# Row lists of 32 experts built in one scatter instead of one one-hot sum per expert

## The chip, the cores and the metric

One core of one Trainium2 chip runs the whole program in one launch. The metric is the device time of the program in microseconds; 1805.8 us is the median of three runs of the kernel before (1805.31 to 1807.24).

## The reference

`reference` is two blocks over 512 tokens of width 1024. The first is a mixer (mLSTM heads and pooling) with a mixture of experts behind it, the second an attention block with spatial gating. The change touches the mixture of experts alone:

```python
logits = (xt @ w_router + b_router).astype(jnp.float32)
top_vals, top_idx = lax.top_k(logits, TOP_K)          # 4 of 32 experts
top_gates = jax.nn.softmax(top_vals, axis=-1)
...
def expert_block(args):
    xb, e = args
    gate = xb @ w_gate[e] + b_gate[e]
    up = xb @ w_up[e] + b_up[e]
    gate = jnp.minimum(gate, SWIGLU_LIMIT)
    up = jnp.clip(up, -SWIGLU_LIMIT, SWIGLU_LIMIT)
    glu = gate * jax.nn.sigmoid(SWIGLU_ALPHA * gate)
    return (glu * (up + 1.0)) @ w_down[e] + b_down[e]
```

Each token's four results are weighted by `top_gates` and summed. Every expert has three 1024 x 1024 float32 matrices, 12 MB in all.

## The kernel before

**Turns.** The experts are sorted by their number of rows, and `vector_order` gives each a place, so that turns alternate between a larger expert (even turn, up to 128 rows) and a smaller one (odd turn, `small(e)`, up to 64 rows). What does not fit is left to `further_blocks`. Turn `e` has 12 pieces of weights of 1 MB: 8 for gate and up, and 4 for down of the expert before.

**A piece.** SyncE loads it into one of five ring slots (`load`, L447) once ScalarE and VectorE have read what was there. ScalarE writes its high part to `WH` (`high`, L1042), VectorE its low part to `WL` (`low`, L1386: ring minus WH, both in SBUF). There are five such pairs of buffers; a buffer is free when TensorE has used it. TensorE multiplies high by high, high by low and low by high; in smaller turns it packs high and low rows into one pass (`rows_by_columns`).

**Rows.** `h2d` in memory holds the 512 normed tokens. `gpsimd_gather(e)` fetches the rows of turn `e` by an indirect DMA into `xg[e % 2]`, with indices from `tok`. TensorE transposes them (`tensor_turn_rows(e)`, L755), ScalarE and VectorE keep them as `xh` and `xl`. `gpsimd_scatter(e)` writes the results by `dst` to `yd`, which has one row for every token and choice.

**Lists of rows.** `P1[token, e]` is the place of the token in the expert's list, plus one, or zero. For a turn `q`, `vector_one_hot(q)` compares `P1` with a row of numbers (four instructions for four blocks of 128 tokens), `tensor_index(q, bank)` multiplies the result with `DV16` (four matmuls of one column, which sum 4 x token + choice + 1), and `vector_index(q, bank)` makes `dst` and `tok` from the sum. Turns 0 to 2 (NI = 3) are done ahead of the loop or in turn 0; later ones, for turn `e + 3`, within turn `e`: the one-hot at piece 2, the matmuls at piece 4 (bank 7, behind a wait for the low part of the transposed hidden rows), the indices at piece 5.

**Order.** Every engine has its own order of instructions, written out by hand; semaphores tie them together. TensorE's is, from the start of the loop: gate and up of turn 0, rows of turn 1, gate and up of turn 1, rows of turn 2, down of turn 0, hidden rows of turn 1, and so on (`tensor_experts`, L875). GpSimd's is (`gpsimd_experts`, L2042): gather 0, biases 0, gather 1, zero and copy `selz`, biases 1 to 3, gather 2, gather 3, scatter 0, gather 4, scatter 1 and so on. VectorE's start is in `vector_experts` (L1716): two low parts with the positions and the one-hots between, the count of what does not fit, the weights `GK`, the fifth low part, then the turns.

Of the kernel before, what the change touches and what calls it, by code (L numbers as in the profile page):

```python
# [73 lines left out]
def program(nc, x, norm1_g, w_in, ig_b, fg_b, conv_w, head_norm_g, pool_w, pool_scale, w_out, norm2_g,  # L74
# [40 lines left out]
    dst = place("dst", [128, E], I32)  # L115
    tok = place("tok", [128, E], I32)
    wc = place("wc", [128, 16], F32)
    fl = place("fl", [128, 16], F32)
    ovm = place("ovm", [128, E, 3], F32)
# [16 lines left out]
    h2d = nc.dram_tensor("h2d", [T, D], F32).ap()  # L136
    b3d = nc.dram_tensor("b3d", [2, 3, E, D], BF16).ap()
    yd = nc.dram_tensor("yd", [T * K, D], F32).ap()
    xv = x[0].rearrange("(j p) d -> p j d", p=128)
    yv = yd.rearrange("(j p k) d -> j p k d", p=128, k=K)  # L140
    ov = out[0].rearrange("(j p) d -> j p d", p=128)
# [88 lines left out]
    bf = ordering("bf", [128, 4], F32)  # L230
    bidx = ordering("bidx", [128, 4], I32)
    foldw = ordering("foldw", [128, HALF], F32R)
    WH += [reg(f"WH{3 + i}", [128, 4, 512], F32R, 53.5 + 16 * i) for i in range(2)]
    WL += [reg(f"WL{3 + i}", [128, 4, 512], F32R, 61.5 + 16 * i) for i in range(2)]

# [185 lines left out]

    t_rows = {e: max(0, 2 * e - 1) for e in range(E)}
    t_mid = {e: 2 * e + 2 if e + 1 < E else 2 * e + 1 for e in range(E)}
    NI = 3
    small = lambda e: e % 2 == 1
    places = lambda e: HALF if small(e) else 128
    fold = {}
# [343 lines left out]

    def tensor_turn_rows(e):
        P.wait_ge(s_xg[e % 2], 16 * (e // 2 + 1))
        P.wait_ge(s_ix, min(e + NI, E) if e else 1)
        if e:
            P.wait_ge(s_tl, t_rows[e])
        else:
            P.wait_ge(s_tall, 16)
        if e == 2:
            P.wait_ge(s_spk, 1)  # L780
        tensor_turn8(xg[e % 2], places(e))
# [34 lines left out]
    def tensor_gate_up(e):  # L816
        P.wait_ge(s_th, t_rows[e] + 1)
        for p in range(8):
            which, kc = p // 4, p % 4
            if p == 0:  # L820
                if e == 0:
                    P.wait_ge(s_lg, 2)
                    P.wait_ge(s_x1, 8)
                else:
                    P.wait_ge(s_eg, e)
            last = rows_by_columns(n_g[e] + p, kc, 2 * which, xh, xl, 0 if p else t_rows[e] + 1, small(e))
            if p == 3:

                if e:
                    P.wait_ge(s_eu, e)  # L830
                else:
                    P.wait_ge(s_bh, 112)
                    P.wait_ge(s_cnt, 1)
                if e == 1:
                    P.wait_ge(s_selz, 2)
                if e == 8:
                    P.wait_ge(s_bh, 160)
                for n in range(4):
                    rows = slice(32 * n, 32 * n + 24)
                    cols = selz[rows, e % 8 // 2] if small(e) else sel8[rows, e % 8:e % 8 + 1].broadcast_to([24, 128])  # L840
                    last = mm(PS[:, n, :], cols, b3[rows, e // 8], n >= 2, n < 2)
            last.then_inc(s_mm, 1)
            if small(e) and p == 1 and e >= 3:
                P.wait_ge(s_low, fold["out", e - 2])
                tensor_fold(4, ysl).then_inc(s_fold, 1)
            if small(e) and p == 6:
                P.wait_ge(s_low, fold["gate", e])
                tensor_fold(0, egl).then_inc(s_fold, 1)
            if p == 1 and e == 1:
                tensor_turn_mid(0)  # L850
            if e == 0 and p + 1 < NI:
                tensor_index(p + 1, 4 + p)
            if p == 4:
                P.wait_ge(s_tl, t_mid[e - 1] + 1 if e else 1)
                if e + NI < E:
                    tensor_index(e + NI, 7)
                if e == 1:
                    P.wait_ge(s_sp, 1)
                    for j in range(4):
                        last = P.transpose(PS[0:32, 6, 128 * j:128 * j + 128], Gt[:, j], ident)  # L860
                    last.then_inc(s_spt, 1)

    def tensor_down(e):
        P.wait_ge(s_th, t_mid[e] + 1)
# [760 lines left out]
        vector_order()  # L1625

    def vector_order():
        V.wait_ge(s_small, 128)
        V.scalar_tensor_tensor(key, cnt, 32.0, late[:, KEYB:KEYB + E], MUL, ADD).then_inc(dv.sem, dv.one())
        for i in range(4):  # L1630
            V.wait_ge(dv.sem, dv.n)
# [26 lines left out]
    def vector_positions():  # L1658
# [3 lines left out]
        V.tensor_copy(cnt, PS[:, 4, 128:160]).then_inc(dv.sem, dv.one())  # L1662
        V.wait_ge(dv.sem, dv.n)

    def vector_further_count():
        V.tensor_tensor(key, cnt, late[:, ADJ:ADJ + E], ADD).then_inc(dv.sem, dv.one())
        V.wait_ge(dv.sem, dv.n)
# [6 lines left out]
        V.tensor_copy(novi, nov[:, 0:1]).then_inc(s_nov, 1)  # L1674

    def vector_one_hot(q):
        if q >= NI:
            V.wait_ge(s_im, q - NI + 1)
        n = places(q)
        for j in range(4):  # L1680
            last = V.tensor_scalar(oh[q % NI][:, j, 0:n], iot16[:, 0:n], P1[:, j, q:q + 1], None, ALU.is_equal)
        last.then_inc(s_oh, 1)

    def vector_index(q, bank):
# [4 lines left out]
        V.scalar_tensor_tensor(dst[0:n, q:q + 1], PS[0:n, bank, 0:1], -1.0, iv[0:n, 0:1], ADD, ADD).then_inc(dv.sem, dv.one())  # L1689
        V.wait_ge(dv.sem, dv.n)  # L1690
        V.tensor_scalar(tok[0:n, q:q + 1], dst[0:n, q:q + 1], 2, None, ALU.arith_shift_right).then_inc(s_ix, 1)  # L1691

    def vector_turn8(t, hi, lo, e):
        V.wait_ge(s_th, t + 1)
# [21 lines left out]
    def vector_experts():  # L1716
# [4 lines left out]
        for q in range(1, NI):  # L1721
            vector_one_hot(q)
        low(first + 3)
        vector_further_count()
        V.wait_ge(s_ek, 1)
        V.reciprocal(sm, sm).then_inc(dv.sem, dv.one())
# [5 lines left out]
        for e in range(E + 1):  # L1732
            if e < E:
                for p in range(8):
# [279 lines left out]
    def gpsimd_routing():  # L2014
        G.tensor_copy(tri16[:, 0], C[:, LTRI:LTRI + 128])
        G.tensor_copy(tri16[:, 1], C[:, ONES:ONES + 128]).then_inc(s_tri, 1)
        G.wait_ge(s_sc, 4)
        G.dma_start(late, cst[:, NC1:NCST]).then_inc(s_small, 16)
        G.tensor_copy(foldw, C[:, IDENT + HALF:IDENT + 128]).then_inc(s_selz, 1)

    def gpsimd_gather(e):
        i = e % 2
        G.wait_ge(s_ix, e + 1)
        if e >= 2:
            G.wait_ge(s_tt, t_rows[e - 2] + 1)
        n = places(e)
        G.indirect_dma_start(xg[i][0:n], None, h2d, bass.IndirectOffsetOnAxis(tok[0:n, e:e + 1], 0), bounds_check=T - 1,  # L2027
                             oob_is_err=False).then_inc(s_xg[i], 16)

    def gpsimd_biases(g):  # L2030
        G.wait_ge(s_sig, 2)
# [4 lines left out]
    def gpsimd_scatter(e):  # L2036
        G.wait_ge(s_ys, e + 1)
        n = places(e)
        G.indirect_dma_start(yd, bass.IndirectOffsetOnAxis(dst[0:n, e:e + 1], 0), ys[e % 2][0:n].rearrange("p h f -> p (h f)"), None,  # L2039
                             bounds_check=T * K - 1, oob_is_err=False).then_inc(s_y[e % 2], 16)  # L2040

    def gpsimd_experts():  # L2042
# [248 lines left out]
```

## Time and profile before

| | us |
|---|---|
| median of three runs | 1805.8 |
| the profiled execution, whole | 1807.08 |
| its span | 1805.7 |
| TensorE matmuls busy | 1684.4 (93%) |
| VectorE busy | 1380.5 (76%) |
| ScalarE busy | 1212.3 (67%) |
| GpSimd busy | 229.4 (13%) |
| VectorE low parts (L1386), 428 | 966.3 |
| ScalarE high parts (L1042), 428 | 814.2 |
| GpSimd gathers of rows (L2027), 32 | 75.3 |
| GpSimd scatters of results (L2039), 32 | 94.6 |

The profile is of one execution, times in microseconds from the start of the span. Its engines are PE (TensorE matmuls), PEld (TensorE weight loads), DVE (VectorE), ACT (ScalarE), POOL (GpSimd) and SP (SyncE, which issues the weight loads). `x32` is a count. `A <- B` behind a wait means that B released A. PEclk is the clock that TensorE was granted, as a share of its full speed. The chain is the work that ended last, followed back from the end of the program. The expert loop runs from about 235 to 1363 us; the mixer lies before it, the second block behind it.

### The profile page before, as it was taken

To read this page: it belongs to the slowest core of one execution; us is meant where nothing else is said; L and a number is where in the kernel's file an instruction comes from. 1 tells how busy PE (TensorE), PEld (TensorE's weight loads), DVE (VectorE), ACT (ScalarE), POOL (GpSimd) and SP (SyncE) were. 2 spreads that over 40 slices of the span, in tenths; PEclk is the share of its full clock that TensorE was granted. 3 is DMA by queue.
4 is the path that set the end of the run, shared out by engine and by line. 5 is a ranking of instruction groups with operands and counts; after the bars stand their busy time and mean duration, and the time that the engine had idled before them with its cause. 6 is when DMAs were issued, how large, how long until landed. Compare 5 with 4: busy or idle time off the path is not lost.

```text
span 1805.7 us, 20193 instructions
## 1 busy us (share of the span) xinstructions
PE 1684.4 (93%) x7609; PEld 1258.7 (70%) x7609; DVE 1380.5 (76%) x1226; ACT 1212.3 (67%) x931; POOL 229.4 (13%) x143
## 2 busy tenths in 40 slices
PE   7999879999999998998989998999988999999998
PEld 5777757676676676676766766766753777778887
DVE  4567689899899989988989998999875524775343
ACT  4354458888888878878888888888873346664232
POOL 1411031022021011210120130122001000000000
PEclk9999979999999999999999999999997999999999
DMA  7311369999999999999999999999985422122221
GB/s 273 126 47 72 134 245 369 393 378 381 388 385 368 376 364 368 386 373 377 355 379 390 367 373 380 364 371 389 378 326 214 140 70 71 47 76 94 94 82 47
DMA packets 94003, 487.99 MB, mean 270 GB/s; under 512 B 12056, under 2 KB 13776, under 8 KB 43984
## 3 DMA queue, kind: packets, MB, share of 16 engines
q1 hardware_dynamic: 81696, 462.64, 67.2%
q0 software_dynamic: 8000, 18.25, 2.8%
q10 hardware_dynamic: 4208, 5.77, 0.9%
q8 instruction: 62, 1.02, 0.2%
q14 instruction: 37, 0.30, 0.0%
HBM read 477.97 MB, written 17.17 MB: 274 GB/s over the span
## 4 chain that ended last, share of the span: by engine, by line
PE 58%; DVE 19%; DMA 8%; issue 8%; ACT 7%; SPq 0%; DVEq 0%; ACTq 0%; POOLq 0%
PE PS L516 52%; DVE WL L1386 12%; DMA ring<-in_w_down_dram 7%; ACT WH L1042 4%; DVE eu L1708 2%; DVE eu L1714 2%; PE PS L977 1%; PE PS L755 1%; DMA ring<-in_w_gate_dram 1%; PE PS L989 1%; ACT eg L1211 1%; ACT eul L1195 1%; DVE xl L1698 1%; DVE xh L1696 1%; PE PS L628 0%
## 5 line engine op out<-in xcount | busy, mean ns | idle before, releaser
L1386 DVE TENSOR_TENSOR WL<-ring,WH 128x2048 fp32r<-128x2048 f32 x428 | 966.3, 2284 | 242.7 <-ACT WH L1042 242.5
L1042 ACT ACTIVATE WH<-ring 128x2048 fp32r<-128x2048 f32 x428 | 814.2, 1913 | 294.1 <-PE PS L516 246.7
L516 PE MATMUL PS<-WH,xh 128*128 128x512 f32 x1024 | 309.1, 403 | 2.2 <-DVE xh L1696 1.5
L516 PE MATMUL PS<-WL,xh 128*64 128x512 f32 (+1 forms) x1024 | 300.9, 398 | 0.0
L516 PEld LDWEIGHTS PS<-WH,xh 128*128 128x128 f32 x1024 | 187.8, 190 | 52.7 <-issue 7.2
L516 PEld LDWEIGHTS PS<-WL,xh 128*64 128x64 f32 (+1 forms) x1024 | 164.0, 164 | 72.4 <-issue 9.0
L2039 POOL DMA_INDIRECT yd<-ys,dst x32 | 94.6, 2956 | 924.3 <-ACT ys L1223 924.3
L516 PE MATMUL PS<-WH,hh 128*128 128x512 f32 x512 | 156.9, 408 | 1.5 <-DVE hh L1696 1.5
L516 PE MATMUL PS<-WL,hh 128*64 128x512 f32 (+1 forms) x512 | 149.4, 399 | 0.0
L516 PE MATMUL PS<-WH,xl 128*128 128x512 f32 x512 | 140.4, 397 | 0.0
L516 PEld LDWEIGHTS PS<-WH,hh 128*128 128x128 f32 x512 | 94.7, 192 | 30.9 <-issue 7.4
L516 PEld LDWEIGHTS PS<-WH,xl 128*128 128x128 f32 x512 | 98.8, 193 | 21.5
L516 PE MATMUL PS<-h,WH 128*128 128x512 f32 x288 | 113.3, 394 | 0.0
L516 PE MATMUL PS<-l,WH 128*128 128x512 f32 x288 | 112.2, 389 | 0.0
L516 PE MATMUL PS<-h,WL 128*128 128x512 f32 x288 | 112.1, 389 | 0.0
L516 PEld LDWEIGHTS PS<-WL,hh 128*64 128x64 f32 (+1 forms) x512 | 84.5, 165 | 33.3
L2027 POOL DMA_INDIRECT xg<-h2d,tok x32 | 75.3, 2353 | 28.0 <-DVE tok L1691 16.2
L516 PE MATMUL PS<-WH,hl 128*128 128x512 f32 x256 | 71.1, 401 | 0.0
L516 PEld LDWEIGHTS PS<-h,WH 128*128 128x128 f32 x288 | 54.1, 188 | 11.7 <-issue 0.2
L516 PEld LDWEIGHTS PS<-h,WL 128*128 128x128 f32 x288 | 54.1, 188 | 11.4
L516 PEld LDWEIGHTS PS<-l,WH 128*128 128x128 f32 x288 | 54.1, 188 | 10.8
L755 PE MATMUL PS<-C,eu 128*128 128x128 f32 (+1 forms) x256 | 38.0, 290 | 22.2 <-DVE eu L1714 12.0
(385 smaller groups left out, 2158.0 us busy)
## 6 DMA issues: line engine op xcount, KB each, us to landing
ring<-in_w_gate_dram SPq DMA_DIRECT2D x128, 1024.0 KB, 8.5
ring<-in_w_up_dram SPq DMA_DIRECT2D x128, 1024.0 KB, 7.1
ring<-in_w_down_dram SPq DMA_DIRECT2D x128, 1024.0 KB, 8.0
ring<-in_w_in_dram SPq DMA_DIRECT2D x32, 1024.0 KB, 5.4
ring<-in_w_out_dram SPq DMA_DIRECT2D x8, 1024.0 KB, 5.0
yk<-yd SPq DMA_DIRECT2D x4, 1024.0 KB, 7.9
X<-in_x_dram SPq DMA_DIRECT2D x4, 512.0 KB, 9.7
h2d<-HV ACTq DMA_DIRECT2D x4, 512.0 KB, 2.8
```

Source lines behind the costliest of these rows:

```text
L516: return P.matmul(ps, a, b, start=start, stop=stop)
L755: last = P.transpose(PS[:, 6 + at_ // 512, at_ % 512:at_ % 512 + n], pairs_[0:n, k // 2, k % 2], ident[0:n, 0:n])
L977: last = P.matmul(flat[:, OFF[i] + 128 * (i2 - i):OFF[i] + 512 - 128 * i], tri[:, 0 if i2 == i else 1], part[:, OFF[i2]:OFF[i2] + 512 - 12 ...
L989: last = P.matmul(flat[:, OFF[i]:OFF[i] + 512 - 128 * i], kT[r0:r0 + 64, ch, 128 * i:128 * i + 128], nq[r0:r0 + 64, ch, 128 * i:512], star ...
L1042: A.activation(WH[buf[n]], ring[spot[n]], ACT.Copy).then_inc(s_hi, 1)
L1195: A.activation(eul[HALF:128], PS[HALF:128, 2:4, :], ACT.Copy).then_inc(s_low, 1)
L1211: A.activation(eg[0:n], PS[0:n, 0:2, :], ACT.Relu, scale=-1.0, bias=C[0:n, LIM:LIM + 1]).then_inc(s_eg, 1)
L1386: V.tensor_tensor(WL[buf[n]], ring[spot[n]], WH[buf[n]].bitcast(F32), SUB).then_inc(s_lo, 1)
L1708: V.tensor_scalar(eu[0:n], PS[0:n, 2:4, :], 7.0, -7.0, MIN, MAX).then_inc(s_eu, 1)
L1714: V.scalar_tensor_tensor(eu[0:n], eu[0:n], 1.0, eg[0:n], ADD, MUL).then_inc(s_eh, 1)
L2027: G.indirect_dma_start(xg[i][0:n], None, h2d, bass.IndirectOffsetOnAxis(tok[0:n, e:e + 1], 0), bounds_check=T - 1, oob_is_err=False).then_ ...
L2039: G.indirect_dma_start(yd, bass.IndirectOffsetOnAxis(dst[0:n, e:e + 1], 0), ys[e % 2][0:n].rearrange("p h f -> p (h f)"), None, bounds_che ...
```

## The change

Indices for turns 0 and 1 are made as before (NI = 2, tiles `dst0` and `tok0`). For turns 2 to 31 they come from one list in memory, `listd`, of 32 x 128 slots with two numbers each (4 x token + choice, and token). It is filled with a number out of bounds ahead of the loop. `vector_slots` works out, for each token and choice, the slot in that list (eight instructions, between the fourth low part and the count). `gpsimd_lists` then scatters the pairs by 16 indirect DMAs of 128 rows of 8 bytes, waits for all, loads the whole list into `lists`, and waits for that. It stands behind the copy of `selz` and ahead of biases 1 to 3. Gathers and scatters of turns 2 to 31 take their indices from `lists`. The one-hots, index matmuls and index instructions in the loop go, and with them the wait at piece 4, except in turn 1, where it stands ahead of the transposes of the weights `Gt`.

```diff
+    listd = nc.dram_tensor("listd", [128 * E, 2], I32).ap()
...
-    NI = 3
+    NI = 2
...
     def tensor_turn_rows(e):
         P.wait_ge(s_xg[e % 2], 16 * (e // 2 + 1))
-        P.wait_ge(s_ix, min(e + NI, E) if e else 1)
+        P.wait_ge(s_ix, min(e + 1, NI))
...
-            if p == 4:
-                P.wait_ge(s_tl, t_mid[e - 1] + 1 if e else 1)
-                if e + NI < E:
-                    tensor_index(e + NI, 7)
-                if e == 1:
...
+            if p == 4 and e == 1:
+                P.wait_ge(s_tl, t_mid[0] + 1)
...
     def vector_order():
-        V.wait_ge(s_small, 128)
+        V.wait_ge(s_small, 144)
...
+    def vector_slots():
+        V.scalar_tensor_tensor(pv, P1, 32.0, C[:, IOTA:IOTA + E].unsqueeze(1).broadcast_to([128, 4, E]), MUL, ADD).then_inc(dv.sem, dv.one())
+        V.tensor_scalar(past, P1, 128.0, 8 * BIG, ALU.is_gt, MUL).then_inc(dv.sem, dv.one())
+        V.tensor_scalar(chosen[:, :, :, 0], C[:, TOKK:TOKK + 16].rearrange("p (j k) -> p j k", j=4), -1.0, None, ADD).then_inc(dv.sem, dv.one())
+        V.wait_ge(dv.sem, dv.n)
+        V.scalar_tensor_tensor(pv, pv, -32.0, past, ADD, ADD).then_inc(dv.sem, dv.one())
+        V.wait_ge(dv.sem, dv.n)
+        V.tensor_tensor(pvk, eqr, pv.unsqueeze(3).broadcast_to([128, 4, E, K]), MUL).then_inc(dv.sem, dv.one())
+        V.wait_ge(dv.sem, dv.n)
+        V.tensor_reduce(slots, pvk.rearrange("p j e k -> p j k e"), AX, ADD).then_inc(dv.sem, dv.one())
+        V.tensor_scalar(chosen[:, :, :, 1], chosen[:, :, :, 0], 2, None, ALU.arith_shift_right).then_inc(dv.sem, dv.one())
+        V.wait_ge(dv.sem, dv.n)
+        V.tensor_copy(sloti, slots).then_inc(s_sig, 1)
...
         low(first + 3)
+        vector_slots()
         vector_further_count()
...
-                    if p == 2 and e + NI < E:
-                        vector_one_hot(e + NI)
-                    if p == 5 and e + NI < E:
-                        vector_index(e + NI, 7)
...
         G.wait_ge(s_sc, 4)
+        G.memset(lists, int(BIG)).then_inc(po.sem, po.one())
+        G.wait_ge(po.sem, po.n)
+        G.dma_start(listd.rearrange("(p s) a -> p (s a)", s=E), lists.rearrange("p s a -> p (s a)")).then_inc(s_small, 16)
         G.dma_start(late, cst[:, NC1:NCST]).then_inc(s_small, 16)
...
     def gpsimd_gather(e):
-        i = e % 2
-        G.wait_ge(s_ix, e + 1)
+        i, n = e % 2, places(e)
+        G.wait_ge(s_ix, min(e + 1, NI))
+        rows = tok0[0:n, e:e + 1] if e < NI else lists[0:n, e, 1:2]
...
+    def gpsimd_lists():
+        G.wait_ge(s_sig, 3)
+        G.wait_ge(s_small, 144)
+        for j in range(4):
+            for k in range(K):
+                G.indirect_dma_start(listd, bass.IndirectOffsetOnAxis(sloti[:, j, k:k + 1], 0), chosen[:, j, k], None,
+                                     bounds_check=128 * E - 1, oob_is_err=False).then_inc(s_small, 16)
+        G.wait_ge(s_small, 400)
+        G.dma_start(lists.rearrange("p s a -> p (s a)"), listd.rearrange("(p s) a -> p (s a)", s=E)).then_inc(s_small, 16)
+        G.wait_ge(s_small, 416)
...
+        gpsimd_lists()
         for g in range(1, 4):
             gpsimd_biases(g)
         for e in range(E + 1):
```

## Rows read from the trace of the kernel before

**Rows 1.** Windows; columns: stretch, length, busy (instructions) by engine, PEclk, DMA share, GB/s.
```profile
core 0: us, PE busy (x) PEld busy (x) DVE busy (x) ACT busy (x) POOL busy (x), PEclk, DMA share, GB/s
233.20:242.10 8.90, 8.11 (x39) 6.30 (x39) 8.33 (x19) 1.19 (x2) 2.89 (x1) 0.50 0.37 129
...
300.20:369.60 69.40, 64.23 (x295) 46.70 (x294) 63.39 (x47) 58.49 (x39) 11.14 (x4) 1.00 0.99 386
...
300.20:1277.70 977.50, 910.99 (x4114) 662.85 (x4113) 888.85 (x638) 805.53 (x519) 157.03 (x56) 0.99 0.97 376
```

**Rows 2.** Chain in order of time, expert loop; columns: start us, us, what.
```profile
300.29 23.04 PE PS L516 x104
...
332.71 8.82 DVE WL L1386 x4
341.65 9.66 DMA ring<-in_w_down_dram
...
447.80 0.59 DVE oh L1681 x4
```

**Rows 3.** Waits, 300 to 1360 us (SP: 230 to 1360); columns: total us, times, longest.
```profile
PE PS L516 <- DVE oh L1681: 17.1, 13, 1.3
...
SPq L450 <- DVE WL L1386: 916.7, 380, 16.3
```

**Rows 4.** Timeline of TensorE; columns: start us, us, engine, line, instruction, operands, count.
```profile
250.69 0.40 PE L516 MATMUL PS<-b,sel 24*128 24x512 bf16 x4
...
286.22 1.20 PE L755 MATMUL PS<-C,xg 128*128 128x128 f32 x8 [0.96 <-ACT GtT L1245]
...
313.62 1.08 PE L516 MATMUL PS<-WH,xl 128*128 128x512 f32 x4
314.63 0.28 PE L516 MATMUL PS<-DV,oh 128*64 128x1 f16 x4
314.85 0.73 PE L516 MATMUL PS<-WH,xh 128*128 128x512 f32 x2
...
316.80 1.07 PE L516 MATMUL PS<-WH,xl 128*128 128x512 f32 x4
317.71 0.61 PE L516 MATMUL PS<-WH,xh 128*128 128x512 f32 x2
```

**Rows 5.** Timeline of GpSimd; in brackets the idle time before and who ended it.
```profile
247.51 2.28 POOL L2027 DMA_INDIRECT xg<-h2d,tok  x1 [10.77 <-DVE tok L1691]
...
252.02 1.07 POOL L2033 DMA_INDIRECT b<-b3d,bidx  x1 [0.17 <-issue]
253.39 4.20 POOL L2033 DMA_INDIRECT b<-b3d,bidx  x1 [0.30 <-issue]
...
259.20 2.39 POOL L2027 DMA_INDIRECT xg<-h2d,tok  x1 [0.30 <-issue]
...
302.93 5.69 POOL L2039 DMA_INDIRECT yd<-ys,dst  x1 [37.36 <-ACT ys L1223]
```

**Rows 6.** Timeline of VectorE, first turns.
```profile
241.33 0.18 DVE L1666 TENSOR_TENSOR key<-cnt,late 128x32 f32<-128x32 f32 x1
...
242.71 0.69 DVE L442 TENSOR_TENSOR e<-eq,GK 128x512 f32<-128x512 f32 x1
...
252.24 4.48 DVE L1386 TENSOR_TENSOR WL<-ring,WH 128x2048 fp32r<-128x2048 f32 x2
258.43 2.29 DVE L1386 TENSOR_TENSOR WL<-ring,WH 128x2048 fp32r<-128x2048 f32 x1 [1.71 <-ACT WH L1042]
...
298.84 8.88 DVE L1386 TENSOR_TENSOR WL<-ring,WH 128x2048 fp32r<-128x2048 f32 x4
```

**Rows 7.** Landing of GpSimd's DMAs: all gathers, the one of 247.51, the load of late.
```profile
DMA to landing us min/median/max: 4.3/10.4/15.6
...
xg<-h2d,tok POOLq DMA_INDIRECT x1, 9.7
...
late<-constants POOLq DMA_DIRECT2D x1, 80.5 KB, 2.3
```

More of the change, by code:

```diff
@@ L114, in program @@
     cnt = place("cnt", [128, E], F32)
-    dst = place("dst", [128, E], I32)
-    tok = place("tok", [128, E], I32)
+    lists = place("lists", [128, E, 2], I32)
     wc = place("wc", [128, 16], F32)
@@ L232, in program @@
     foldw = ordering("foldw", [128, HALF], F32R)
+    dst0, tok0 = (ordering(n, [128, 2], I32) for n in ("dst0", "tok0"))
+    slots = ordering("slots", [128, 4, K], F32)
+    sloti = ordering("sloti", [128, 4, K], I32)
+    chosen = ordering("chosen", [128, 4, K, 2], I32)
+    pv = reg("pv", [128, 4, E], F32, 16)
+    past = reg("past", [128, 4, E], F32, 16.5)
+    pvk = reg("pvk", [128, 4, E, K], F32, 17)
     WH += [reg(f"WH{3 + i}", [128, 4, 512], F32R, 53.5 + 16 * i) for i in range(2)]
@@ L852, in tensor_gate_up @@
                 tensor_index(p + 1, 4 + p)
-            if p == 4:
-                P.wait_ge(s_tl, t_mid[e - 1] + 1 if e else 1)
-                if e + NI < E:
-                    tensor_index(e + NI, 7)
-                if e == 1:
[L858 to L861, printed above, removed]
+            if p == 4 and e == 1:
+                P.wait_ge(s_tl, t_mid[0] + 1)
+                P.wait_ge(s_sp, 1)
+                for j in range(4):
+                    last = P.transpose(PS[0:32, 6, 128 * j:128 * j + 128], Gt[:, j], ident)
+                last.then_inc(s_spt, 1)
     def tensor_down(e):
@@ L1676, in vector_one_hot @@
     def vector_one_hot(q):
-        if q >= NI:
-            V.wait_ge(s_im, q - NI + 1)
         n = places(q)
@@ L1688, in vector_index @@
         V.wait_ge(dv.sem, dv.n)
-        V.scalar_tensor_tensor(dst[0:n, q:q + 1], PS[0:n, bank, 0:1], -1.0, iv[0:n, 0:1], ADD, ADD).then_inc(dv.sem, dv.one())
+        V.scalar_tensor_tensor(dst0[0:n, q:q + 1], PS[0:n, bank, 0:1], -1.0, iv[0:n, 0:1], ADD, ADD).then_inc(dv.sem, dv.one())
         V.wait_ge(dv.sem, dv.n)
-        V.tensor_scalar(tok[0:n, q:q + 1], dst[0:n, q:q + 1], 2, None, ALU.arith_shift_right).then_inc(s_ix, 1)
+        V.tensor_scalar(tok0[0:n, q:q + 1], dst0[0:n, q:q + 1], 2, None, ALU.arith_shift_right).then_inc(s_ix, 1)
     def vector_turn8(t, hi, lo, e):
@@ L2021, in gpsimd_gather @@
     def gpsimd_gather(e):
-        i = e % 2
-        G.wait_ge(s_ix, e + 1)
+        i, n = e % 2, places(e)
+        G.wait_ge(s_ix, min(e + 1, NI))
+        rows = tok0[0:n, e:e + 1] if e < NI else lists[0:n, e, 1:2]
         if e >= 2:
             G.wait_ge(s_tt, t_rows[e - 2] + 1)
-        n = places(e)
-        G.indirect_dma_start(xg[i][0:n], None, h2d, bass.IndirectOffsetOnAxis(tok[0:n, e:e + 1], 0), bounds_check=T - 1,
+        G.indirect_dma_start(xg[i][0:n], None, h2d, bass.IndirectOffsetOnAxis(rows, 0), bounds_check=T - 1,
                              oob_is_err=False).then_inc(s_xg[i], 16)
+    def gpsimd_lists():
+        G.wait_ge(s_sig, 3)
+        G.wait_ge(s_small, 144)
+        for j in range(4):
+            for k in range(K):
[4 more added lines that the diff above has]
+        G.wait_ge(s_small, 416)
     def gpsimd_biases(g):
@@ L2038, in gpsimd_scatter @@
         n = places(e)
-        G.indirect_dma_start(yd, bass.IndirectOffsetOnAxis(dst[0:n, e:e + 1], 0), ys[e % 2][0:n].rearrange("p h f -> p (h f)"), None,
+        G.indirect_dma_start(yd, bass.IndirectOffsetOnAxis(dst0[0:n, e:e + 1] if e < NI else lists[0:n, e, 0:1], 0), ys[e % 2][0:n].rearrange("p h f -> p (h f)"), None,
                              bounds_check=T * K - 1, oob_is_err=False).then_inc(s_y[e % 2], 16)
```

## The prediction

> **What bounds the kernel now.** I read four views in this order. First the windows [rows 1]: from 300.2 to 1277.7 us, 28 turns of the expert loop, TensorE is busy 911 of 977.5 us and the DMA engines 0.97 of the time. One pair of turns (an expert of up to 128 rows, then one of up to 64) takes 69.4 us, with TensorE busy 64.2 us, VectorE 63.4 and the DMA engines 0.99. Three resources are nearly full, so being busy decides nothing. Second the chain in order of time [rows 2]: in a pair it stands for 23.0 us on TensorE (gate and up of the larger expert), later for 8.8 us on four low parts that VectorE makes back to back, then for 9.7 us on the load of a `w_down` piece. Third the waits [rows 3]: the queue that loads weights waits 380 times for a low part, because a ring slot is only free when VectorE has read it. The loop is therefore a ring: load, high part on ScalarE, low part on VectorE, matmuls, next load; it has little slack and no idle stretch in which something of 20 us could hide. Fourth the timelines of the first two turns [rows 4 to 6], since the change puts new work there.
>
> **What goes away, turn by turn.** For experts 3 to 31 the old kernel makes a one-hot (four VectorE instructions), sums it with four matmuls of one column in bank 7, and turns the sum into indices (three more). That is 29 turns, and the one for expert 2 as well. What does it cost on TensorE? Where no index comes between two pieces, the next piece begins 0.91 us after the last group's first matmul (316.80 to 317.71); with the index matmuls between, it is 1.23 us (313.62 to 314.85) [rows 4]. So 0.32 us per turn. On top, TensorE waits for the one-hot in 13 turns of the smaller kind, 17.1 us in all [rows 3]. If everything came through, 29 x 0.32 + 17.1 = 26.4 us would be saved. But the chain passes such a turn of the smaller kind by the low parts and the load of `w_down`, not by TensorE [rows 2]: an earlier TensorE only waits longer for its next weights. What lies on the chain is the index group of each larger turn, inside the 23.04 us, 14 x 0.32 = 4.5 us, and the one-hot on VectorE in three places, 0.6 to 0.8 us each (the shortest of them in [rows 2]), 2.3 us together. I take 7 us, with 0 (the DMA engines, at 0.99, take it back) and 26 as bounds. The wait at p == 4 for the last low part goes too; that part is VectorE's work of pieces before, so I price it at nothing; if it ever was last, it is within the 26.
>
> **What VectorE gets at the start.** `vector_slots` is eight instructions ahead of the fifth low part: two over 512 elements per partition like the ones for the weights (0.69 us each [rows 6]), the rest over 128 elements or less at some 0.2 us, together 2.7 us. The list of slots is then ready at 241.3 [rows 6] - 0.6 (one one-hot less) + 2.7 = 243.4 us. The fifth low part starts at 246.1 instead of 244.0, and the index of expert 1 is ready at 248.8 instead of 246.7. TensorE wants that low part only behind the biases of 250.7 [rows 4], so VectorE itself delays nothing. What it does change is who waits behind it on GpSimd.
>
> **How GpSimd issues while VectorE makes low parts.** An indirect DMA on GpSimd takes 1.0 us when VectorE is not in a low part, with 0.3 us to the next (252.02). Otherwise it ends 0.9 us after the end of the run of low parts that it met: VectorE's run 252.24 to 256.72, GpSimd's issue 253.39 to 257.59; the run 298.84 to 307.7, GpSimd's issue 302.93 to 308.62 [rows 5, 6]. The low parts start 2.20 us apart and leave no hole. I therefore take GpSimd as shut out for whole runs. The Trainium skill, page "SBUF — State Buffer", section "Who interferes with whom", says that a VectorE instruction with two SBUF inputs holds up GpSimd's reads, which this trace agrees with, but infers for `tensor_tensor` that descriptor generation is not stalled, which the rows just named contradict; that rule's outcome is the first rival below.
>
> **What is put on GpSimd's queue and who waits behind it.** The old queue has, after the gather for expert 1, three bias gathers, then the gather for expert 2, issued at 259.2 us; TensorE turned those rows at 286.2 us without waiting for them [rows 4]. Now 16 scatters, a wait for all of them, a load of the whole list, a wait for that, and the bias gathers stand ahead of the gather for expert 2. Behind that gather stand TensorE's transposes of expert 2, and behind these, in its own order, the down product of expert 0. Step by step:
> - Gather for expert 1: asked for at 248.8, but without one-hots and indices VectorE now runs four low parts in one run to 257.6. It ends at 258.5. Its rows took 9.7 us with an issue of 2.3 us in it, so 7.4 us after its end [rows 5, 7]: 265.9 instead of before 262.6, when TensorE wants them: 3.3 us of waiting.
> - The copy of `selz` reads SBUF and comes behind the next run, 264.4. The scatters begin at 264.7.
> - VectorE stands still until expert 1's rows are turned (268.5) and then does one reading from PSUM, so 5 scatters get out by 271. From there until TensorE stops at about 290 it makes low parts almost without a hole: two or three scatters more; with the last holes until 297, when its buffers are full, 10 are out. Six are left at 1.3 us: 305.
> - No trace row shows 8-byte rows scattered. Bounds for landing: 2.3 us (the load of `late`) and 13.6 us (longest gather, 15.6, less the issue). The weight queue is empty by then, so I take 3.3 us, the shortest gather (4.3) less its issue: 308.5. The list's load: 0.6 + 2.6 = 3.2, so 311.7. Three bias gathers at 1.3: 315.6. The gather: 4.3 at the least, 10.4 at the median under load [rows 7]; unloaded but behind the bias rows, I take 4.7: 320.3 us.
>
> So TensorE turns expert 2's rows at 320.3 instead of 286.2: **34 us** later. Bounds: 14 (first rival) and 57 (third).
>
> **What follows the stall.** TensorE has stood still 30 us. After its wait before the loop (5.9 us) its granted clock was 0.50, i.e. 1.2 GHz, for 8.9 us in which it was busy 8.1 us [rows 1]; at 2.4 GHz that work takes half. So +4.0 us. On the other hand the loads run on until all ring slots are full; three pieces of 2.8 us (1 MB at the 386 GB/s of [rows 1]) are then ahead, and the 9.7 us on `w_down` vanish from the chain in the next pairs. What a pair could gain at most is its 5.2 us without TensorE; the head start is 8.4 us. I take 6 us back (0 to 8.4). Later gathers of the list have no new wait, and the rest of the kernel is untouched.
>
> **Sum.** The profiled execution took 1807.1 us (span 1805.7 and 1.4 around it), 1.3 over the median of the three runs. 1807.1 + 34 + 4 - 6 - 7 = 1832.1; against the median 1831. I predict **1831 us**.
>
> **Rivals.**
> - *GpSimd is not shut out* (the rule quoted above says so). The scatters begin at 252.5: 16 x 1.3 = 20.8, 273.3; landing under load 7.4, 280.7; list 0.6 + 5, 286.3; biases 3.9, 290.2; gather 9.7, 299.9. Stall 14 us, no wait for expert 1, slower clock some 2 us, little head start (3): 1807.1 + 14 + 2 - 3 - 7 = 1813. Against it: every issue above 1.1 us in [rows 5] ends 0.9 us after a run. For it: GpSimd might only need the port once for several instructions in a row.
> - *Faster.* The time freed on TensorE and VectorE reaches the end in every turn: with VectorE's seven instructions per turn gone, the low parts and so the loads come sooner, and the 26.4 us are saved in full. Its place is each turn from expert 0 to 28. It decides from the point where the start costs less than 26 us net: with the first rival's start, 1807.1 + 14 + 2 - 3 - 26.4 = 1794. Against it: the chain rarely holds the removed instructions, and the DMA engines are at 0.97 to 0.99. With my own start it gives 1813, still slower.
> - *The list comes much later.* Each scatter costs what indirect issues cost on average among low parts, 2.39 us (252.02 to 261.59 for four): 264.7 + 38.2 = 302.9, landing 13.6, list 8, biases 7.2, gather 10.4: 342.1. Stall 56: 1854. For it: small rows in memory are something that no row shows.
> - *The change saves nothing per turn*, because loads set the pace: 1838.
>
> **How the numbers follow.** My case, with or without the saving per turn (1820 to 1843): 0.66. First rival: 0.12 (1806 to 1820). The late list: 0.13. Faster: 0.06, and 0.03 for a mixture that lands at no change. The range from 1808 to 1850 leaves out the faster case and most of the late list. A difference of 0.2% (3.6 us) is about what a measurement of this kernel can tell from none. Faster 0.06, same 0.04, slower 0.90.
>
> **What would show it.** In the changed profile: 16 scatters on GpSimd between about 264 and 305 us, the first ones and the last ones 1.3 us apart, those between with gaps of several low parts; a wait of TensorE for `xg` of some 30 us near 290, after one of about 3 near 263; a fall of the granted clock behind it; DMA at rest for over 20 us near 300; pairs of turns from then on at 69 us or a little less, the first ones after the stall shortest. I would be wrong if the scatters went out evenly at 1.3 us, if 8-byte rows took much longer to land, or if the pairs fell by 1.5 us and more.

## The result and the profile after

The changed kernel took 1820.1 us (median of four runs, 1817.5 to 1821.3), the kernel before 1805.6 in the runs beside it. The ratio is 1.0081, with a 95% interval from 1.0061 to 1.0101: slower by 11 to 18 us. Its profiled execution has a span of 1819.9 us, 14.2 more than before.

The first turns on GpSimd, from the timeline of the changed kernel (start us, us, engine, line, instruction, operands, count, idle time before):

```profile
249.41 8.89 POOL L2043 DMA_INDIRECT xg<-h2d,tok  x1 [12.75 <-DVE tok L1707]
...
258.90 1.57 POOL L2080 COPY selz<-sel 128x256 bf16<-128x256 bf16 x1
260.65 2.88 POOL L2051 DMA_INDIRECT listd<-chosen,sloti  x1 [0.18 <-issue]
263.84 1.00 POOL L2051 DMA_INDIRECT listd<-chosen,sloti  x1 [0.30 <-issue]
...
274.56 1.90 POOL L2051 DMA_INDIRECT listd<-chosen,sloti  x1 [0.30 <-issue]
276.76 1.90 POOL L2051 DMA_INDIRECT listd<-chosen,sloti  x1 [0.30 <-issue]
278.96 3.03 POOL L2051 DMA_INDIRECT listd<-chosen,sloti  x1 [0.30 <-issue]
...
291.10 0.98 POOL L2051 DMA_INDIRECT listd<-chosen,sloti  x1 [0.30 <-issue]
297.09 0.58 POOL L2054 DMA_DIRECT2D lists<-listd  x1 [5.00 <-DMA listd<-chosen,sloti]
303.40 1.06 POOL L2060 DMA_INDIRECT b<-b3d,bidx  x1 [5.73 <-DMA lists<-listd]
...
307.37 1.00 POOL L2043 DMA_INDIRECT xg<-h2d,lists  x1 [0.30 <-issue]
```

The 16 scatters are issued from 260.7 to 292.1 us, without a pause between them but the 0.3 us from one to the next. Then come 5.0 us until the last has landed, 0.6 and 5.7 us for the list, 4.0 us for three bias gathers, and the gather for turn 2. What it did to TensorE (transposes of the rows of turns 1 and 2, L755 in [rows 4], L762 here):

```profile
266.23 1.22 PE L762 MATMUL PS<-C,xg 64*128 64x64 f32 x8 [4.50 <-DMA xg<-h2d,tok]
...
312.07 1.98 PE L762 MATMUL PS<-C,xg 128*128 128x128 f32 x8 [23.79 <-DMA xg<-h2d,lists]
```

Turn 2's rows come 25.9 us later than the 286.2 us of [rows 4], behind a wait of 23.8 us. The chain of the work that ended last goes the same way, through GpSimd and its transfers to TensorE (columns as in [rows 2]):

```profile
249.41 8.89 POOL xg L2043
...
288.90 1.90 POOL listd L2051
291.10 0.98 POOL listd L2051
...
297.09 5.52 DMA lists<-listd
...
307.37 4.66 DMA xg<-h2d,lists
312.07 1.98 PE PS L762 x8
```

Four windows show the loop around it, to be read beside [rows 1]:

```profile
core 0: us, PE busy (x) PEld busy (x) DVE busy (x) ACT busy (x) POOL busy (x), PEclk, DMA share, GB/s
226.00:300.00 74.00, 48.86 (x220) 35.99 (x220) 60.85 (x78) 41.89 (x28) 42.42 (x22) 0.80 0.72 270
300.00:366.00 66.00, 53.16 (x233) 40.73 (x234) 41.82 (x23) 38.77 (x25) 10.26 (x7) 0.87 0.67 253
302.00:310.00 8.00, 0.00 (x0) 0.00 (x0) 0.00 (x0) 0.00 (x0) 5.00 (x5) 0.50 0.29 75
310.00:322.00 12.00, 9.93 (x36) 7.82 (x37) 1.73 (x1) 3.07 (x3) 0.00 (x0) 0.71 0.13 44
```

In the 66 us from 300 us the DMA engines move 253 GB/s in place of 385 in the same stretch of the kernel before. The weight loads don't stop with TensorE: they go on until about 302 us, and then nearly rest for some 20 us. The loop never gets that time back in full. The table gives, for some turns, how much later than in the kernel before TensorE began to transpose their rows, read from the timelines of the profiled executions (us; minus is earlier; the kernels E1 to E5 follow below). The last column is the difference of the spans. Each row is one execution: that of E2 was the slowest of its six, 4.9 us above their median, that of E3 4.9 us below the median of its twelve, the others, the kernel before too, lie within 1.5 us of theirs.

| turn | 1 | 2 | 4 | 10 | 16 | 24 | 31 | span |
|---|---|---|---|---|---|---|---|---|
| changed | 3.6 | 25.9 | 25.6 | 23.3 | 22.9 | 14.6 | 16.0 | 14.2 |
| E1 four ahead | -0.5 | 2.3 | 2.0 | 5.9 | -0.8 | -5.3 | -5.8 | -4.6 |
| E2 list unused | 3.1 | 29.3 | 32.0 | 35.2 | 31.1 | 27.1 | 27.0 | 27.4 |
| E3 biases behind | 3.1 | 20.5 | 20.8 | 19.8 | 15.2 | 7.3 | 4.9 | 0.5 |
| E4 removal alone | 0.7 | 0.8 | -1.7 | 0.4 | -3.6 | -11.0 | -8.8 | -13.5 |
| E5 slots later | -1.6 | -0.1 | -1.0 | 0.2 | -3.6 | -8.7 | -11.0 | -10.6 |

The loss of the changed kernel is all there by turn 3 (27.6 us). Of it 11.6 us are won back by turn 31 and 13.4 by the end of the span. One line of its waits from 300 to 1363 us answers to [rows 3] (no wait for a one-hot is left; columns: total us, times, longest):

```profile
PE PS L776 <- ACT eul L1199: 47.3, 15, 5.4
```

In the kernel before, the same wait, for the low rows of up, was this:

```profile
PE PS L769 <- ACT eul L1195: 27.7, 15, 4.2
```

The 17.1 us of one-hot waits of [rows 3] are gone, and this wait is 19.6 us longer.

### The profile page after: what moved, and what is told of

It reads as the page before. It is cut to its first block, busy times and chain, and to the rows that moved or that the text cites. A ratio compares the mean times of both kernels' runs of the same rounds, so it can differ in the third digit from the quotient of the medians.

```text
span 1819.9 us, 19756 instructions
## 1 busy us (share of the span) xinstructions
PE 1684.0 (93%) x7489; PEld 1267.1 (70%) x7489; DVE 1355.6 (74%) x1024; ACT 1213.8 (67%) x931; POOL 275.4 (15%) x162
## 4 chain that ended last, share of the span: by engine, by line
PE 61%; DVE 14%; DMA 9%; issue 8%; ACT 6%; POOL 2%; SPq 0%; POOLq 0%; ACTq 0%; DVEq 0%
PE PS L523 55%; DVE WL L1390 9%; DMA ring<-in_w_down_dram 7%; ACT WH L1046 3%; PE PS L981 1%; POOL listd L2051 1%; DVE eu L1724 1%; PE PS L762 1%; DVE eu L1730 1%; PE PS L993 1%; ACT eul L1199 1%; ACT eg L1215 1%; PE PS L776 1%; DMA ring<-in_w_gate_dram 1%; DVE xh L1712 1%
## 5 line engine op out<-in xcount | busy, mean ns | idle before, releaser
L523 PE MATMUL PS<-WL,xh 128*64 128x512 f32 (+1 forms) x1024 | 295.0, 395 | 0.0
L2066 POOL DMA_INDIRECT yd<-ys,lists x30 | 77.5, 2583 | 825.7 <-ACT ys L1227 825.7
L523 PE MATMUL PS<-WH,hh 128*128 128x512 f32 x512 | 164.8, 425 | 2.2 <-DVE hh L1712 2.2
L523 PE MATMUL PS<-WL,hh 128*64 128x512 f32 (+1 forms) x512 | 159.5, 421 | 0.0
L523 PEld LDWEIGHTS PS<-WH,hh 128*128 128x128 f32 x512 | 98.8, 201 | 33.5 <-issue 10.4
L523 PEld LDWEIGHTS PS<-WL,hh 128*64 128x64 f32 (+1 forms) x512 | 90.5, 177 | 36.3 <-issue 1.2
L523 PEld LDWEIGHTS PS<-WH,xl 128*128 128x128 f32 x512 | 96.7, 189 | 20.5
L2043 POOL DMA_INDIRECT xg<-h2d,lists x30 | 99.9, 3329 | 9.1 <-issue 9.1
L762 PE MATMUL PS<-C,xg 128*128 128x128 f32 (+1 forms) x256 | 38.3, 295 | 34.0 <-DMA xg<-h2d,lists 23.8
L762 PEld LDWEIGHTS PS<-C,xg 128*128 128x128 f32 (+1 forms) x256 | 35.4, 212 | 41.3 <-DMA xg<-h2d,lists 24.2
L523 PEld LDWEIGHTS PS<-WH,hl 128*128 128x128 f32 x256 | 53.9, 211 | 13.0
```

What stands on the lines that cost most here:

```text
L523: return P.matmul(ps, a, b, start=start, stop=stop)
L762: last = P.transpose(PS[:, 6 + at_ // 512, at_ % 512:at_ % 512 + n], pairs_[0:n, k // 2, k % 2], ident[0:n, 0:n])
L2066: G.indirect_dma_start(yd, bass.IndirectOffsetOnAxis(dst0[0:n, e:e + 1] if e < NI else lists[0:n, e, 0:1], 0), ys[e % 2][0:n].rearrange("p ...
```

## The experiments

The yardstick is the kernel before on the same chip: 1805.6 us for E1 to E4, 1802.4 for E5 to E8, 1805.5 for E9 to E12. Single runs of one kernel spread over 10 to 25 us there, so ratios with their intervals are compared, not medians of different chips.

**E1: the list off TensorE's path.** Turns 0 to 3 get their indices as before, from one-hots; the list is made behind their gathers.

```diff
-    NI = 2
+    NI = 4
...
-        P.wait_ge(s_ix, min(e + 1, NI))
+        P.wait_ge(s_ix, NI if e else 1)
...
+        gpsimd_gather(2)
+        gpsimd_gather(3)
         gpsimd_lists()
...
-            if e + 2 < E:
+            if 4 <= e + 2 < E:
                 gpsimd_gather(e + 2)
```

> The changed kernel, but the indices of turns 0 to 3 are made by one-hots ahead of the loop, and the 16 scatters stand behind the gather for turn 3, so no gather waits for the list before turn 4, which TensorE reaches some 60 us later than the list can be there. Theory A (the whole loss is TensorE's wait for the rows of turn 2 and what it does to the clock; the removed instructions are worth about 0.75 us per pair of turns for good): no wait for gathered rows above 2 us, and 1792 to 1797 us, 9 to 13 below the kernel before. Rival B (the 11 us that the changed kernel makes up between turn 4 and the end are only its loads' head start out of the stall, the removal itself is worth nothing): 1803 to 1807 us. Rival C (the 16 small scatters and the list load slow the weight loads wherever they stand): 1810 or more, with a fall of the DMA rate near 270 to 320 us.

Measured: 1801.3 us, ratio 0.9965 (0.9941 to 0.9989). No wait for gathered rows is left, and the version is faster than the kernel before, by 2 to 11 us. That rules out C and speaks against B, whose 1803 to 1807 would be no gain, though its interval touches B's edge. It is also short of theory A's 1792 to 1797. The trace shows a longer wait for the weights `GtT` at turn 2's transposes (0.96 us in [rows 4]):

```profile
288.54 1.72 PE L762 MATMUL PS<-C,xg 128*128 128x128 f32 x8 [4.56 <-ACT GtT L1249]
```

**E2: the list alone.** The kernel before, with slots, scatters, list load and waits where the changed kernel has them, and nobody using the list.

```diff
         low(first + 3)
+        vector_slots()
         vector_further_count()
...
+        gpsimd_lists()
         for g in range(1, 4):
             gpsimd_biases(g)
```

> The kernel before with the list added: slots on VectorE, 16 scatters, the load of the list and its waits at the same places as in the changed kernel, but nobody uses the list, all per-turn one-hots and index matmuls stay. Theory A (the stall is lost for good, and the removal is worth about 11 us): TensorE turns the rows of turn 2 some 26 us later, and the time is 1826 to 1832 us, 9 to 12 above the changed kernel. Rival B (the loads' head start makes up some 11 us whatever is removed): 1817 to 1822 us, as the changed kernel.

Measured: 1829.5 us, ratio 1.0121 (1.0097 to 1.0144), 22 us over the kernel before (18 to 26). That is theory A's time, and not B's 1817 to 1822. TensorE waits 26.9 us for turn 2's rows, and the table's lag is 32 us at turn 4 and 27 at the end. In that execution about 5 us of the stall come back by themselves. It was the slowest of the six, though; by the ratio it would be 6 to 14 us, if the other executions lost the same 32 us at the start.

**E3: four microseconds less in the chain.**

```diff
         gpsimd_lists()
+        gpsimd_gather(2)
+        gpsimd_gather(3)
         for g in range(1, 4):
             gpsimd_biases(g)
...
-            if e + 2 < E:
+            if 4 <= e + 2 < E:
                 gpsimd_gather(e + 2)
```

> The changed kernel with the three bias gathers moved behind the gathers of turns 2 and 3, which then stand 3.9 us earlier on GpSimd (the issues took 303.4 to 307.4 us in the changed kernel). Theory A (what TensorE waits for is GpSimd's serial chain, one to one): the wait for the rows of turn 2 falls from 23.8 to 19 to 20 us, and the time by 3 to 5 us, to 1815 to 1817 us. Rival B (a later constraint of the loads takes it back, the wait's length doesn't matter to the end): the wait falls but the time stays within 1 us of the changed kernel.

Measured: 1812.4 us, ratio 1.0043 (1.0022 to 1.0064). The wait for turn 2's rows, from the waits of this kernel (total us, times, longest):

```profile
PE PS L762 <- DMA xg<-h2d,lists: 19.1, 1, 19.1
```

It is 4.7 us shorter than the changed kernel's 23.8, and the ratio falls by 0.0038, 7 us, give or take 5. That speaks for theory A, by which what stands on GpSimd ahead of that gather costs about its own length, and against rival B, by which the time would stay within 1 us. The time itself came out below the 1815 to 1817 us that theory A gave.

**E4: the removal alone.** There is no list and there are no slots. Turns from 2 on gather and scatter with the indices of turns 0 and 1, and the combination at the end reads weights in place of the results, so this version leaves out the right rows.

```diff
-        rows = tok0[0:n, e:e + 1] if e < NI else lists[0:n, e, 1:2]
+        rows = tok0[0:n, e % NI:e % NI + 1]
...
-        gpsimd_lists()
```

> The changed kernel without the list: no slots, no scatters, no list load; turns from 2 on gather and scatter with the indices of turns 0 and 1, and the combination at the end reads weights in place of results, so the right rows are left out, with the same instructions and bytes otherwise. It is the removal alone. Theory A: 1792 to 1797 us, with the offset to the kernel before growing by about 0.75 us per pair, TensorE's wait for a one-hot gone but its wait for the low part of up longer by nearly as much. Rival B (removal is worth nothing, the loads set the pace): 1803 to 1807 us. Rival D (all that is freed on TensorE arrives): 1779 to 1783 us.

Measured: 1794.4 us, ratio 0.9936 (0.9913 to 0.9959), 7 to 16 us faster. That is theory A, with the wait for the low rows of up at 51.6 us; B (1803 to 1807) and D (1779 to 1783) are out. The parts add up: +22 (E2) and -12 (E4) make +10, against the +14.5 of the changed kernel, within what the intervals allow.

**E5 and E11: the slots later.** E1 with one more move.

```diff
         low(first + 3)
-        vector_slots()
...
+                    if e == 0 and p == 4:
+                        vector_slots()
```

> The version with four turns' indices ahead and the list behind the gather of turn 3, with the slots moved on VectorE from ahead of the fifth low part into turn 0, behind its piece 4, where VectorE stands idle for 1.7 us before the next high part. In the version without that move the fifth low part starts at 247.2 instead of 244.0 us, the DMA rate from 236 to 262 us is 239 instead of 292 GB/s, and TensorE waits 4.6 us near 288. Theory A (VectorE's 3 us ahead of the fifth low part delay the freeing of ring slots, and so the loads): the rate there comes back to 270 to 290 GB/s, the wait near 288 falls below 2 us, and the time is 1793 to 1798 us where the kernel before has 1805.6, 3 to 6 less than with the slots ahead (ratio 0.9935 to 0.996). Rival B (the start is not what keeps that version from the 1794 us of the removal alone, but the scatters that go out beside the loads): 1800 to 1803, ratio 0.997 to 0.9985.

> The version with four turns ahead and the slots later, unaltered, as the yardstick for the one with zero matmuls. All theories: 1793 to 1800, a ratio of 0.994 to 0.998 to the kernel before.

The windows of E1, of E5 and of the kernel before, in this order, from 236 to 262 us (columns as in [rows 1]):

```profile
236.00:262.00 26.00, 25.99 (x112) 19.85 (x112) 25.42 (x50) 15.33 (x10) 11.81 (x5) 0.90 0.69 239
```

```profile
236.00:262.00 26.00, 26.00 (x120) 20.18 (x120) 25.42 (x50) 16.54 (x10) 10.74 (x5) 0.94 0.77 290
```

```profile
236.00:262.00 26.00, 25.65 (x110) 19.73 (x111) 23.52 (x42) 16.82 (x11) 13.66 (x8) 0.88 0.79 292
```

The loads run at 239 GB/s with the slots ahead of the fifth low part, at 290 with them later (283 in E11), so those instructions on VectorE do hold up the loads where nothing else stalls. But the wait at turn 2 only falls from 4.6 to 3.8 us (2.5 in E11), not below 2 as theory A wanted; what keeps it is open. In the end time this isn't separated: 1797.1 us and 0.9961 (0.9939 to 0.9983) in E5, 1795.7 us and 0.9943 (0.9919 to 0.9966) in E11, against E1's 0.9965. This is the version that beats both kernels, the one before by about 0.5%.

**E6 and E7: which half of the removal counts.** Both start from E4 and leave out the right rows as it does. E6 puts VectorE's instructions back:

```diff
+                    if p == 2 and e + 3 < E:
+                        n = places(e + 3)
+                        for j in range(4):
+                            last = V.tensor_scalar(oh[2][:, j, 0:n], iot16[:, 0:n], P1[:, j, e + 3:e + 4], None, ALU.is_equal)
```

and three small instructions at piece 5. E7 puts TensorE's matmuls and the wait at piece 4 back:

```diff
+            if p == 4 and e + 3 < E:
+                P.wait_ge(s_tl, t_mid[e - 1] + 1 if e else 1)
+                n = places(e + 3)
+                for j in range(4):
+                    mm(PS[0:n, 7, 0:1], oh[1][:, j, 0:n] if small(e + 3) else oh[0][:, j, 0:n], DV16[:, j, e + 3:e + 4], j == 0, j == 3)
```

> The removal alone, with VectorE's seven instructions per turn put back (they compare and count into tiles that nobody reads), TensorE's four matmuls and both waits still gone. As in the removal alone, turns from 2 on use the lists of turns 0 and 1 and the combination reads weights, so the right rows are left out. The removal alone was 1794.4 against 1805.6. Theory A (TensorE's matmuls and waits were what cost): 1795 to 1798. Rival B (the ring of loads passes through VectorE, so its 1.2 us per turn are what cost): 1801 to 1805.

> The removal alone, with TensorE's four matmuls of one column per turn and its wait for the last low part put back, but no wait for a one-hot, and VectorE's instructions still gone. The same parts are left out as in the removal alone. Theory A (TensorE's 0.32 us in each larger turn lie on the chain): 1798 to 1801, 4 to 7 above the removal alone. Rival B (VectorE carries it): 1794 to 1796.

Measured: E6 1809.9 us, ratio 1.0031 (1.0009 to 1.0054); E7 1801.2 us, ratio 0.9993 (0.9969 to 1.0016). E6, above both of its theories, leaves none of the removal's 0.64%, and E7 leaves 0.31% at most. So "TensorE's part is what costs" (A in E6) and "VectorE carries it" (B in E7) are both out, and neither pair of theories had the two results together. In E7 the wait at piece 4 never ends last (no such line is among TensorE's waits from 300 to 1363 us), so of what E7 puts back only the four matmuls are left to count. My reading is that TensorE and VectorE are so close to each other in the loop that freeing one alone mostly moves the wait to the other. That is argued, not shown. In E6 the wait for the low rows of up is 57.9 us, where the kernel before has 27.7 and 17.1 for one-hots. That E6 comes out slower than the kernel before, which has more work, I can't explain; E10 tries one reason.

**E8: the changed kernel again**, on the chip of E5 to E7.

> The changed kernel unaltered, on the same chip as the other three, as their yardstick. All theories: 1819 to 1822 where the kernel before has 1805.6, a ratio of 1.007 to 1.009, with TensorE's waits for the rows of turns 1 and 2 at about 4.5 and 24 us again.

Measured: 1822.2 us, ratio 1.0113 (1.0063 to 1.0163), a little above what was expected but with an interval that holds 1.0081. TensorE waits 4.4 us for the rows of turn 1 and 24.5 us for those of turn 2, as expected.

**E9, E10, E12: TensorE's clock behind the longer wait.** The piece of down behind the wait for the low rows of up, in the kernel before and then in the changed kernel:

```profile
358.48 0.68 PE L769 MATMUL PS<-eul,foldw 64*64 64x512 f32 x2 [1.85 <-ACT eul L1195]
359.08 0.73 PE L516 MATMUL PS<-WH,hh 128*128 128x512 f32 x2
359.65 0.63 PE L516 MATMUL PS<-WL,hh 128*128 128x512 f32 x2
...
361.04 1.08 PE L516 MATMUL PS<-WH,hl 128*128 128x512 f32 x4
```

```profile
384.20 0.68 PE L776 MATMUL PS<-eul,foldw 64*64 64x512 f32 x2 [2.09 <-ACT eul L1199]
384.80 0.86 PE L523 MATMUL PS<-WH,hh 128*128 128x512 f32 x2
385.47 1.05 PE L523 MATMUL PS<-WL,hh 128*128 128x512 f32 x2
...
388.03 1.39 PE L523 MATMUL PS<-WH,hl 128*128 128x512 f32 x4
```

In the changed kernel the pairs of matmuls take 1.05 in place of 0.63 us. The granted clock is 0.50 from 385.4 to 388.0 us (1.2 GHz), and 1.00 from 359.0 to 362.0 us in the kernel before (2.4 GHz). The piece takes 4.45 in place of 2.9 us. Of the 15 such pieces behind a first one without a wait, it is long (over 3.9 us) in all 15, in the kernel before in 5. That gives back about 10 x 1.6 = 16 us of TensorE's time. Does it reach the end? Eight matmuls by zeros fill the wait, in E5's version (E9), in E6's (E10) and in the kernel before (E12). `zz` is a tile of zeros that GpSimd makes ahead of the loop, and what they add to the down sum is zero.

```diff
+                for _ in range(8):
+                    mm(PS[:, 4, :], zz, hh[:, 0:4].rearrange("p k t -> p (k t)"), False, False)
                 P.wait_ge(s_low, fold["up", e + 1])
```

> The version with four turns ahead and the slots later, with eight more matmuls of 128x512 by a tile of zeros (they add nothing to the down sum) behind the first down piece of each larger expert, where TensorE otherwise stands still for 2 to 5 us until ScalarE has kept the low rows of up. In the changed kernel, and in all versions without the index matmuls, the piece behind that wait takes 4.4 us in nearly all of 15 turns, against 2.86 us in 10 of 15 turns of the kernel before; the granted clock from 350 to 1270 us is 0.97 or less against 0.99. Theory F (part of what the removal frees is given back there, since TensorE's standing still in one piece lowers its clock, and that lies on the way to the end): the piece takes 2.9 us in at least 12 of 15 turns, the clock is 0.99 or more, and the time is 4 to 12 us below the same version without them, 1785 to 1793. Rival G (the clock falls but what it costs is hidden, since the loads set the pace): the pieces get short, the time stays within 2 us, or rises by 1 to 4 us where the eight matmuls reach past the wait.

> The removal alone with VectorE's seven instructions put back, which took 1809.9 where the kernel before had 1802.4, and the same eight zero matmuls in each larger expert's down. The same parts are left out as in the removal alone. Theory F (that version was slower than the kernel before, which has strictly more work, because its TensorE stands still in one piece and its clock falls in 14 of 15 turns): 1797 to 1803. Rival G (hidden): 1808 to 1812.

> The kernel before with the eight zero matmuls in each larger expert's down. There the piece behind the wait took 4 us or more in 5 of 15 turns. Theory F: those turns get short as well, 3 to 6 us below the kernel before. Rival G: no difference, or 1 to 4 us more.

Windows from 350 to 1270 us, of the version without the fill (E11) and with it (E9), columns as in [rows 1]:

```profile
350.00:1270.00 920.00, 868.55 (x3826) 641.08 (x3825) 827.42 (x429) 773.37 (x498) 183.42 (x54) 0.97 0.98 383
```

```profile
350.00:1270.00 920.00, 880.03 (x3956) 651.96 (x3955) 830.19 (x432) 773.05 (x498) 213.99 (x54) 0.99 0.98 384
```

The granted clock is back at 0.99 and the piece is long in 2 of 15 turns, so the fill does what it should. The time doesn't follow: E9 1796.2 us, ratio 0.9955 (0.9928 to 0.9983), against E11's 0.9943. So the fill costs 2 us, give or take 7, and at most 5 of the 4 to 12 us that theory F gave can be there. The rate of the loads is the same, 384 and 383 GB/s. E12 took 1805.0 us, ratio 1.0014 (0.9986 to 1.0042), with long pieces in 1 of 15 turns; F's gain of 3 to 6 us lies outside that interval. So rival G holds: what the clock costs there is hidden. The gain turns into other waits: from 350 to 1270 us ScalarE waits 44.2 us for loads of weights in E9, 28.3 in E11, and for TensorE 97.9 us in place of 113.7.

E10 took 1807.0 us, ratio 1.0005 (0.9980 to 1.0030), with long pieces still in 8 of 15 turns (14 in E6). It falls between what F and G gave, and its interval overlaps E6's. So the clock isn't shown to be E6's reason; E10 itself can't be told from the kernel before.

## Why the prediction was right or wrong

- **Forecast 1831, measured 1820.1**, inside the range, slower as forecast. The net change was put at +25 and is +14.2 in the profiled executions. The result lies on the line between what I gave my own case (1820 to 1843) and the first rival (1806 to 1820).
- **The mechanism held**: GpSimd's serial chain ahead of the gather for turn 2, TensorE waiting for those rows from 288 us on, the loads at rest from about 302 us. E1 and E2 show it from both sides: the list off the path is 2 to 11 us faster than before, the list alone 18 to 26 us slower.
- **The stall's length is the term that was mis-sized**: 34 us forecast, 25.9 measured. The step that failed is "I therefore take GpSimd as shut out for whole runs" of low parts. The runs were there, from VectorE's timeline of the changed kernel:

```profile
271.11 6.69 DVE L1390 TENSOR_TENSOR WL<-ring,WH 128x2048 fp32r<-128x2048 f32 x3
277.72 1.22 DVE L1714 TENSOR_TENSOR hl<-PS,hh 128x1024 fp32r<-128x1024 f32 x1
278.86 11.09 DVE L1390 TENSOR_TENSOR WL<-ring,WH 128x2048 fp32r<-128x2048 f32 x5
```

  But in them one scatter went out with each low part, 1.90 us for an issue and 2.20 from one to the next. The copy of `selz` wasn't held up to the end of its run either (260.5, not 264.4). So the last scatter was out at 292.1 instead of 305. Both rows that the rule came from (253.39 and 302.93 in [rows 5]) did show a whole run; two were too few. In the other direction, landing took 5.0 us (3.3 forecast) and the list 6.3 (3.2). The biases (4.0) and the last gather with its landing (4.7) were as forecast.
- **Turn 1's rows**: 265.9 forecast, 266.2 measured. There the gather did wait for the whole run of four low parts, 8.89 us.
- **The clock after the stall**: +4.0 forecast. The first down piece and the transposes took 2.2 us more than before (the lag grows from 25.9 to 28.0 us by the second piece). I had priced the whole low stretch ahead of the loop, 8.9 us; here the granted clock is 0.50 from 312 to 316 us and 0.88 from 316 to 320.
- **What comes back**: 6 from the loads' head start and 7 from the removal, 13 in all; 13.4 measured from turn 3 to the end. That the sum fits is in part luck. The removal alone is worth 12 us, 7 to 16 (E4), within the bounds of 0 and 26 but above the 7 taken. From turn 3 to turn 31 the changed kernel wins back 11.6 us and E4 wins 9.1, most of it between turns 16 and 24 in both (8.3 and 7.3), long after the stall. That leaves 2.5 us for the head start, not 6, and the pairs right behind the stall weren't those that won most. E2, without any removal, gives back 5 us in its profiled execution. How much a head start is worth stays open within these numbers.
- **Why so little of the 26 us**: as argued, an earlier TensorE waits elsewhere: the 17.1 us of waits for one-hots went over into the wait for the low rows of up. But the prices by part were wrong in kind. I had put 4.5 us on TensorE and 2.3 on VectorE, as if they added. By E6 and E7, TensorE's half alone is worth nothing and VectorE's half at most 0.31%, 5.6 us.
- **VectorE's start, priced at nothing**: the slots took 3.0 us, 2.7 forecast. From 236 to 262 us the loads fall from 292 GB/s in the kernel before to 261 in the changed kernel, and to 239 in E1, which has the one-hots of two more turns ahead of the same low part. In the changed kernel the stall comes behind and can cover that. The prediction should have named it; its price in the end time is too small to be told by E1 and E5.
- **The rivals**: the rival "not shut out" (1813) comes nearer, 7 us below the result where the main case is 11 above, and the trace stands between the two. What the Trainium skill infers in "SBUF — State Buffer", section "Who interferes with whom", that `tensor_tensor` doesn't stall descriptor generation, doesn't fit here: an issue took 1.90 to 8.89 us beside VectorE's low parts against 0.98 without one. "Saves nothing per turn" falls with E4. "The list comes much later" falls with the timeline, the last scatter being out at 292.1 us and not 302.9. "Faster" falls with the result, and its 26.4 us with E4's 12.
- **The signs**: the scatters stand between 260.7 and 292.1 us (264 to 305 forecast), the waits are 4.5 and 23.8 us (3 and 30), and the loads nearly rest for some 20 us as forecast. From turn 4 to turn 24 a pair of turns takes 68.8 us, 69.9 in the kernel before, a fall of 1.1 us, short of the 1.5 that would have spoken against the prediction.
- **Slips in the sums**: 305 and 3.3 make 308.3, not 308.5; the late list's stall is 56 in one place and 57 in another; 1838 is told against the median, 1813, 1794 and 1854 against the profiled execution, 1.3 us higher. None changes a reading.

## What to carry to other kernels

Work that is moved from every turn to the start pays its whole serial chain there: add up issue, landing, reload and all that stands behind it on the same queue, and compare with the moment when the next engine needs its result. Keep the old way for as many turns as that chain lasts, and put the new one behind their requests. In a loop where several engines are nearly full, price a removal for all of them together; the part on one engine may be worth little alone, as in E6 and E7.

## What the runs showed of the hardware that was not expected

- **GpSimd and runs of low parts.** Sixteen scatters of 128 rows of 8 bytes mostly went out one to a low part, but not always. In E2 two of them waited for whole runs (E1 and E5 have one issue each of 8.56 us); the timelines of GpSimd and of VectorE in E2:

```profile
256.40 6.39 POOL L2061 DMA_INDIRECT listd<-chosen,sloti  x1 [0.31 <-issue]
...
281.69 6.95 POOL L2061 DMA_INDIRECT listd<-chosen,sloti  x1 [0.30 <-issue]
```

```profile
255.23 6.69 DVE L1394 TENSOR_TENSOR WL<-ring,WH 128x2048 fp32r<-128x2048 f32 x3
...
281.09 6.69 DVE L1394 TENSOR_TENSOR WL<-ring,WH 128x2048 fp32r<-128x2048 f32 x3
```

  They end at 262.8 and 288.6, 0.9 us after the runs. In these first turns of the changed kernel and of E2 the held-up issues end 0.8 to 1.0 us after the end of a low part, and one in each (272.05 and 271.44 us) after the end of `eu<-eu,eg`, which has both inputs in SBUF as well. Which low part an issue gets in behind, the next or the last of the run, stays open. The size of the rows doesn't decide it, since the same kind of scatter did both.
- **Small rows cost as much to issue as large ones**: with VectorE not in the way, 0.98 us for 128 rows of 8 bytes, 0.91 to 1.1 us for rows of 1 and 4 KB.
- **TensorE's clock** fell in all 15 such pieces of the changed kernel, behind waits of 2.0 to 5.4 us. The length of the wait alone doesn't decide it: in the kernel before it stayed up behind waits of 2.62 us (at 636 us) and 2.20 us (at 707 us) and fell behind one of 1.82 us (at 988 us), and in E4 it fell behind one of 1.68 us. Keeping it up with matmuls by zeros bought no time that these runs can tell, with the DMA engines busy at 0.98.
